# Projections of all token blocks grouped on one weight tile, with one weight load for the group

## The reference

```python
h = rmsnorm(x, norm1_g);  z = h @ w_in            # columns [zb | zc | zv | zu | ga | gs]
ya = zb * conv3_causal(zc * zv)                   # 512 channels
ys, state = s5(zu)                                # diagonal complex state space, 32 groups of 16 channels
gy = gelu(ys);  ys = gy * sigmoid(gy @ w_glu + b_glu)
m = sigmoid(ga) * (ya @ wb_conv) + sigmoid(gs) * (ys @ wb_ssm)
x = x + m @ w_out
h2 = rmsnorm(x, norm2_g);  gate, up = split(h2 @ w_gate_up, 2)
x = x + (silu(gate) * up) @ w_down                # 2816 hidden channels
```

## Time and profile before

| | |
|---|---|
| median of 3 runs | 3663.75 us (3659.91 to 3669.96) |
| profiled execution | 3665.26 us |
| its span, slowest core (core 3) | 3663.7 us |
| spans of the 8 cores | 3647.5 to 3663.7 us, mean clock 0.981 to 0.985 |
| PE busy (matmuls) | 3504.0 us, 96% of the span, 23912 instructions |
| PEld busy (weight loads) | 1979.7 us, 54%, 23912 instructions |
| DVE (VectorE), ACT (ScalarE), POOL (GpSimd) | 44%, 31%, 17% |
| chain that ended last | PE 88%, of which line 669 (`proj`) 83% |

### The profile page before, as it was taken

One profiled execution on the slowest core, in us unless ns is written; L12 is line 12 of the kernel. 1 busy time (PEld: TensorE's weight loads), 2 busy tenths in 40 slices (PEclk: granted clock), 3 DMA queues, 4 the chain that ended last, 5 costly groups with the idle time before them and its releaser, 6 DMA issues.

```text
span 3663.7 us, 67385 instructions; the slowest of 8 cores (3647.5 to 3663.7 us)
## 1 busy us (share of the span) xinstructions
PE 3504.0 (96%) x23912; PEld 1979.7 (54%) x23912; DVE 1618.6 (44%) x2889; ACT 1141.7 (31%) x2151; POOL 608.7 (17%) x799
## 2 busy tenths in 40 slices
PE   6699999999999999999999899999999999999998
PEld 3466666666666666666664344444444444444443
DVE  8745555465454654543244331354224442254313
ACT  4443234332353322533134320243103421042202
POOL 4232210322103221030000200002000110002000
PEclk9799999999999999999999999999999999999999
DMA  7444557435574355854338544574445644474443
GB/s 157 115 82 70 114 139 149 87 66 113 138 155 86 62 113 135 185 110 84 70 71 196 116 77 71 98 169 74 75 77 115 144 70 81 70 146 79 79 72 87
DMA packets 252804, 384.14 MB, mean 105 GB/s; under 512 B 157632, under 2 KB 180800, under 8 KB 246848
## 3 DMA queue, kind: packets, MB, share of 16 engines
q0 software_dynamic: 67968, 243.30, 39.5%
q1 hardware_dynamic: 184512, 136.53, 12.8%
HBM read 567.06 MB, written 56.12 MB: 170 GB/s over the span
## 4 chain that ended last, share of the span: by engine, by line
PE 88%; DVE 4%; issue 3%; DMA 3%; ACT 1%; SPq 1%; DVEq 0%; ACTq 0%; POOL 0%; POOLq 0%
PE ps L669 83%; DMA yT<-X 1%; PE ps L702 1%; PE ps L1107 1%; DVE SC L561 1%; DVE H L726 1%; PE ps L1033 1%; PE ps L908 1%; PE ps L1080 0%; DVE X L1246 0%; DMA scv<-CIN 0%; SPq L632 0%; PE ps L895 0%; DMA X<-xsT 0%; DVE R L1225 0%
## 5 line engine op out<-in xcount | busy, mean ns | idle before, releaser
L669 PE MATMUL ps<-H,RING 128*128 128x512 bf16 (+2 forms) x12160 | 2194.9, 340 | 23.5 <-DVE H L726 9.7
L669 PEld LDWEIGHTS ps<-H,RING 128*128 128x128 bf16 x12160 | 1191.5, 99 | 965.9 <-issue 52.3
L669 PE MATMUL ps<-R,RING 128*128 128x384 bf16 (+2 forms) x6400 | 1162.1, 339 | 19.7 <-DMA R<-dy 11.4
L669 PEld LDWEIGHTS ps<-R,RING 128*128 128x128 bf16 x6400 | 624.2, 98 | 517.8 <-issue 35.4
L656 POOL DMA_DIRECT2D RING<-wpk x472 | 253.0, 537 | 2635.0 <-PE ps L669 2431.7
L1268 DVE TENSOR_TENSOR R<-SC,ps 128x384 bf16<-128x384 f32 (+2 forms) x440 | 255.8, 583 | 786.7 <-PE ps L669 773.6
L1267 ACT ACTIVATE SC<-ps 128x384 f32<-128x384 f32 (+2 forms) x440 | 226.1, 515 | 1208.0 <-PE ps L669 1199.6
L1246 DVE TENSOR_TENSOR X<-X,ps 128x384 f32<-128x384 f32 (+2 forms) x480 | 269.8, 582 | 448.2 <-PE ps L669 445.2
L700 ACT ACTIVATE H<-X 128x384 bf16<-128x384 f32 (+2 forms) x304 | 156.6, 539 | 198.4 <-DVE X L1246 178.7
L726 DVE SCALAR_TENSOR_TENSOR H<-X,PRM,SC 128x384 bf16<-128x384 f32 (+2 forms) x304 | 183.0, 672 | 35.0 <-ACT SC L707 34.8
L1240 POOL TENSOR_TENSOR R<-TB,SC 128x384 bf16<-128x384 f32 (+1 forms) x160 | 168.1, 1063 | 113.1 <-DVE SC L1237 101.4
(11 more groups left out here) (180 smaller groups left out, 1633.1 us busy)
## 6 DMA issues: line engine op xcount, KB each, us to landing
RING<-wpk POOLq DMA_DIRECT2D x440, 512.0 KB, 7.0
TAB<-stash SPq DMA_DIRECT2D x21, 1792.0 KB, 10.0
stash<-TAB SPq DMA_DIRECT2D x15, 1792.0 KB, 7.6
R<-stash SPq DMA_DIRECT2D x7, 1792.0 KB, 14.8
RING<-wpk POOLq DMA_DIRECT2D x32, 384.0 KB, 6.1
du<-R SPq DMA_DIRECT2D x32, 256.0 KB, 9.2
UU<-du SPq DMA_DIRECT2D x32, 256.0 KB, 7.2
dy<-YY SPq DMA_DIRECT2D x32, 256.0 KB, 6.6
```

The source lines that it names most:

```text
L669: subs.append((lambda e, u=u, kw=kw, c=c, src=src, i=i: e.matmul(ps[:, 0:blk.n], lhsT=u.ap(kw, c), rhs=src(blk), start=(i == 0), stop=(i = ...
```

## The change

`proj` takes a list of blocks. For each weight tile it runs the matmuls of all these blocks one after the other: the first in the usual way, with a load, the others through `keep`, which issues a matmul that is told not to load. Each block has a PSUM buffer of its own, and all of them belong to one operation of the scheduler. The planned durations change: `MMW` for a product of one block, `MMK` for matmuls of a group.

All products use the whole list of blocks (`joint`) but for four: zu of the first two row tiles and the first fg/fu unit of a layer go block by block (`split`), and so do wo and the second part of fd. In the convolution, all blocks of zv come first, then all of zc; all of gs come before all of wbb.

```diff
 MMN = lambda n: max(64, n + 6) / 2400.0
+MMW = lambda n: n / 2400.0 + 0.0092 + max(0, 512 - n) * 4.6e-5
+MMK = lambda n: n / 2400.0 + 0.0035
...
-    def proj(parts, blk):
-        ps = PP.new()
+    def keep(e, out, lhsT, rhs, start, stop):
+        return e.add_instruction(mybir.InstMatmult(
+            start_tensor_calc=start, stop_tensor_calc=stop, tile_size=(128, 128), tile_position=(0, 0), ldweights=False,
+            name=nc.get_next_instruction_name(), engine=mybir.EngineType.PE, ins=[e.lower_ap(rhs), e.lower_ap(lhsT)], outs=[e.lower_ap(out)]))
+
+    def proj(parts, bl):
+        pss = [PP.new() for _ in bl]
         nmm = len(parts)
         subs = []
         for i, (u, kw, c, src, keys) in enumerate(parts):
...
+            for bi, blk in enumerate(bl):
+                ps = pss[bi]
+                if bi == 0:
+                    fn = lambda e, u=u, kw=kw, c=c, src=src, i=i, ps=ps, blk=blk: e.matmul(
+                        ps[:, 0:blk.n], lhsT=u.ap(kw, c), rhs=src(blk), start=(i == 0), stop=(i == nmm - 1))
+                else:
+                    fn = lambda e, u=u, kw=kw, c=c, src=src, i=i, ps=ps, blk=blk: keep(
+                        e, ps[:, 0:blk.n], u.ap(kw, c), src(blk), i == 0, i == nmm - 1)
+                subs.append((fn, [u.key] + keys(blk), MMW(blk.n) if len(bl) == 1 else MMK(blk.n)))
+        S.pe(subs, [(ps,) for ps in pss], FULL)
+        return pss
...
         blks = BLKS[half]
+        joint = [blks]
+        split = [[b] for b in blks]
...
             u = next_unit("zu")
+            for bl in (split if f0 == 0 else joint):
+                for mt in range(2):
+                    f = 2 * f0 + mt
+                    for blk, ps in zip(bl, projh(u, mt, bl)):
...
-                    pc, pv = projh(uc, mt, blk), projh(uv_, mt, blk)
+                pvs = projh(uv_, mt, rb_)
+                pcs = projh(uc, mt, rb_)
+                for blk, pc, pv in zip(rb_, pcs, pvs):
...
-                for mt in range(2):
+                for bl, mt in [(b_, m_) for b_ in (split if t0 + pr == 0 else joint) for m_ in range(2)]:
                     ti = slots[2 * pr + mt]
-                    for blk in blks:
+                    for blk, pg, pu in zip(bl, projh(ug, mt, bl), projh(uu, mt, bl)):
```

More of the change, by code:

```diff
@@ L1155, in gas @@
                 t_ = tj[jj] = TP.new()
-                for blk in blks:
-                    pg = projh(uga[jj // 2], jj % 2, blk)
+                for blk, pg in zip(blks, projh(uga[jj // 2], jj % 2, blks)):
                     act(lambda e, t_=t_, pg=pg, blk=blk: e.activation(out=t_[:, blk.c0:blk.c0 + blk.n], in_=pg[:, 0:blk.n], func=AF.Sigmoid),
@@ L1166, in layer @@
                 cin = CP.new()
[L1167 removed]
+                rb_ = blks[::-1]
+                pvs = projh(uv_, mt, rb_)
+                pcs = projh(uc, mt, rb_)
+                for blk, pc, pv in zip(rb_, pcs, pvs):
                     n = blk.n
[L1169 removed]
                     iv = SP_.new()
@@ L1183, in layer @@
                     S.dma("sp", lambda e, cin=cin, f=f: e.dma_start(out=scv[l, :, 64 + 16 * f:80 + 16 * f], in_=cin[:, 1152:1168]), [(cin, 8)], [], 8192)
-                for blk in reversed(blks):
+                pbs = projh(ub, mt, rb_)
+                for blk, pb in zip(rb_, pbs):
                     n, npr = blk.n, blk.np
@@ L1208, in layer @@
                 j = 4 * j4 + jj
-                for blk in blks:
+                for blk, po in zip(blks, projr(uwa, jj * 128, [YA + k for k in range(4)], blks)):
                     n = blk.n
-                    po = projr(uwa, jj * 128, [YA + k for k in range(4)], blk)
                     t_ = tj[jj]
@@ L1217, in layer @@
                 for mo in range(4):
-                    for blk in blks:
+                    for blk, pg in zip(blks, projr(ug, mo * 128, [YS + k for k in range(4)], blks)):
                         n = blk.n
-                        pg = projr(ug, mo * 128, [YS + k for k in range(4)], blk)
                         sg = SP_.new()
@@ L1230, in layer @@
                 j = 4 * j4 + jj
-                for blk in blks:
+                for blk, pg, po in zip(blks, projh(ugs[jj // 2], jj % 2, blks), projr(uwb, jj * 128, [UT + k for k in range(4)], blks)):
                     n = blk.n
-                    pg = projh(ugs[jj // 2], jj % 2, blk)
-                    po = projr(uwb, jj * 128, [UT + k for k in range(4)], blk)
                     sg = SP_.new()
@@ L1273, in layer @@
                     for mt in range(2):
-                        for blk in blks:
-                            parts = [((ua, ub)[k // 8], k % 8, mt * 128, rsrc(slots[k]), rk(slots[k])) for k in range(16)]
-                            xadd(proj(parts, blk), 2 * jq + mt, blk)
+                        parts = [((ua, ub)[k // 8], k % 8, mt * 128, rsrc(slots[k]), rk(slots[k])) for k in range(16)]
+                        for blk, ps in zip(blks, proj(parts, blks)):
+                            xadd(ps, 2 * jq + mt, blk)
             else:
```

17 lines of the change are left out of this document (4 added, 13 removed).

## The result

The changed kernel takes 3776.84 us (median of 4 runs, 3755.2 to 3821.22), the kernel before on the same chips 3665.45; ratio 1.0275, 95% interval 1.0207 to 1.0343. The forecast was 3720 with a range to 3760: the sign was right, the size was not.

The account below looks back on a forecast made before the run. TensorE's stream and its waits were taken as the bound, with loads already hidden. Terms 0 + 19 + 16.5 + 15 + 5.4 + 6 + 4 - 7 - 5 = 53.9 us on 3665.3 gave 3719, say 3720 us; range 3660 to 3760.

Parts of the forecast that it names:

- More half clock: Expected sign: more stretches of TensorE at granted clock 0.50, behind new waits such as those at the norms.
- Loads removed: 9216 matmuls without a load, each saving 0 to 2.6 ns: 0 to 24 us, taken as 0.
- the first rival: Loads do cost, so their removal outweighs the waits from 5.9 ns a matmul; 8.5 ns gives 3642 us; chance 0.12.
- Norm n1, second half: First product behind the norm waits for H tiles with 8 matmuls of cover, not 32: 3 x 5.5 = 16.5 us lost.
- Norm n1, first half: 32 cover matmuls before the third block's first product go; waits for H and half clock: 3 x 6.3 = 19 us.
- State space: Layers 2 to 4: waits for VT, 15 us in the first half; lost gate-matmul cover, 5.4 us in the second.
- wo: At its start, waits for the first block's tile since the last merge product signals once: 8 x 0.7 = 6 us.
- Norm n2, first half: At an existing wait of TensorE, cover shrinks from 64 to 56 matmuls: 1.3 us, three times, 4 us lost.
- Second half, first layer: Wait for the last round's result before glu is covered by 56 matmuls instead of 16: 7 us gained.
- Instruction supply: Waits without a releaser shrink with 9216 instructions fewer: 5 us gained, bounds 0 and 14.
- the start: Start-up, where VectorE sets the pace with the same work: 0, with 10 us either way.
- The third rival: Waits chain up: late table load for the fourth state space round, more half clock; 3754 us, chance 0.18.

Follow-up runs that it names:

- E1: Changed kernel with every matmul loading its weights again, same order and plan; 3760.18 to 3766.78 us, ratio to the kernel before 1.0222.
- E2: Changed kernel with both zu tile pairs, the first products behind norm n1, block by block, all else grouped; ratio to the kernel before 1.0157.
- E3: Changed kernel with the gate and convolution products block by block, all else grouped; ratio to the kernel before 1.0254.
- E5: Changed kernel with GpSimd's next-layer table work started only when norm n2's last H tile is written; ratio to the kernel before 1.0237.
- E8: Changed kernel with the planned matmul durations as before the change, groups kept; ratio to the kernel before 1.0204.
- E7: Changed kernel with the glu products and the merge block by block; ratio to the kernel before 1.0218.
- E4: Grouping in the feed-forward products alone, all else in the order and with the planned durations of the kernel before; ratio to it 1.003.
- E11: Grouping in the feed-forward alone, old planned durations, GpSimd's table work started behind norm n2; ratio to the kernel before 1.0011.
- E12: E11 with groups of at most two blocks; lowest time 3646 us, profiled time 3653 us, -18 and -20 us against the kernel before.
- E10: Changed kernel with old planned durations and with zu, gate and convolution products block by block; ratio to the kernel before 1.0228.

## Why the sign was right and the size wrong

The two lowest runs, 3755.2 and 3757.97 us, lie just inside the range; the loss is still 1.8 times the one that was added up, and two of its terms failed. More half clock, which was forecast, came: the mean granted clock is 0.983 in before (median core) and 0.974 on cores 4 to 7 of the changed kernel.

**Loads removed, 0 of a possible 24: right** (E1: at most 7), and with it falls the first rival. The 25 ns a load, the estimate from the Trainium skill (TensorE: Matmul & The Clock Gate, "Back-to-back issue gap"), do not show at these widths.

**Norm n1, second half, 16.5: right**, 16 us came back in E2. **Norm n1, first half, 19: the wait was there** (2.2 us on line 739 in each layer, then a product drawn out over the tiles), but taking it away returns only 9, since the convolution is the next to be late.

**State space, 15 + 5.4: the waits were there, near the size.** VT waits on core 5 rose from nothing to 13.1 us in half 1, and from 6.5 to 15.1, by 8.6, in half 2. But the covers are not independent: grouping zu alone accounts for 5 of the 13.1 (E2 has 7.7), and E3 takes waits for H away. The norm and the state space together, half 1's layers 2 to 4: 19 + 15 and 2 of wo make 36 predicted, 42 measured; half 2's: 24 predicted, 26 measured.

**wo, 6: 9.0 measured** (eight waits, 1.3 us at most), within its bounds.

```profile
PE ps L679 <- POOL R L1254: 9.0, 8, 1.3
```

**Norm n2, first half, 4: failed.** With the feed-forward and the norm n1 behind it, it is 23.0 - 15.1 + 8.5 = 16.4 us. The step counted matmuls of cover and took the H tiles' durations from the trace of before. It left out that the order of VectorE and GpSimd would move, and that the duration of an H tile depends on what GpSimd does. E5 and E8 both remove the new wait of 6.4 us. E8 does it by the planned durations alone and takes all of the 16.4 back (the three rows are at -3.2), so grouping alone does not cause this loss; the new durations without the groups were not run. The change's two new duration functions had no term in the sum at all; undoing them returns 14 to 22 us. The wait that the step did name, for the third block's H, was 3.2 us in before (core 4, first line) and 4.9 in E8 (core 0, second line), 1.7 longer where 1.3 were forecast; in the changed kernel, behind the new wait, it was 1.5 (core 5).

```profile
PE ps L669 <- DVE H L726: 3.2, 2, 2.4
PE ps L679 <- DVE H L739: 4.9, 2, 3.9
```

**Second half, first layer, -7: failed**, +10.8 measured (-1 to 13 by core). The wait for the last round's result did shrink, by 3.8 us only, from 13.5 to 9.7. The step put the 56 matmuls into the gap and counted no new wait at the places they left. There are such waits now, for the convolution (line 1219), for Y's results (line 1131) and others, and glu itself waits 4.1 us for its sigmoids, where the granted clock is 0.50 (2110 to 2120 us on core 5). E7 shows that the sigmoids' wait and the round's trade one for one; that the others come from the matmuls that moved is argued, not shown.

**Instruction supply, -5:** waits without a releaser on core 5 fell from 13.0 to 9.7 us in the layers behind the first, -3.

The misses: 16.4 - 4 = 12; 10.8 + 7 = 18; 42 - 36 = 6, 26 - 24 = 2; 2 to 3 each at the start, the change of half and the rest, which had 0, together 7; and 5 for the supply, which had no place of its own, so that its gain lies inside these rows. That makes 50, where 101 - 54 = 47 were missing (wo's 1.4 us in the two first layers and the rounding of medians are the difference). The third rival, waits that chain up, has the sign and nearly the time (3754), but by luck: the table load it named shows in no wait of TensorE on core 5.

Open: why layer 4 of half 1 loses 13 to 16 us in E4, E11 and E12 (R comes late by its transfer, 5.6 us in E11, and instruction supply, 3.4), and why fine and coarse products side by side cost layers of half 1 in E3 and E10. That a group keeps its banks longer is supported for the feed-forward alone, by E12, where VectorE's list moved as well.

## What to carry to other kernels

Before saving an instruction, show that it is on the path: if a matmul takes the same 2.6 ns over its columns at three widths, with a load of 98 ns that fills 45% of its time at 512 columns and 84% at 272, the load is hidden there, and what its removal does to the order is the larger part. In a program that a planner orders, every number that the planner reads is an edit of its own: change durations and grouping apart, and compare by stages, since E3's sum of zero was some 50 us won and 55 lost. And look at what a cover is made of: rows of matmuls ahead of a norm, and also free banks, which groups of three use up six at a time.

## What the runs showed of the hardware

Beside GpSimd's work some of VectorE's instructions take much longer: here only ones with all operands in SBUF, and not all of those. Over the eight cores of the changed kernel, instructions alone and with over 80% of their time beside a GpSimd tensor_tensor (median ns, count):

```
scalar_tensor_tensor, 384 columns, X to H (SBUF)    612 (822)     1614 (62)
scalar_tensor_tensor, 272 columns, X to H (SBUF)    496 (434)     1307 (72)
tensor_tensor, 384 columns, one operand in PSUM     549 (2482)     547 (86)
tensor_scalar, 256 columns, one operand (SBUF)      293 (40)      1065 (88)
tensor_tensor, 512 columns, TB to SC (SBUF)         691 (993)      693 (83)
```

The Trainium skill (GPSIMD Engine Reference, "1. Specifications") says that GpSimd shares its SBUF interfaces with VectorE, and that they contend when VectorE's instruction is in a 2-port perf mode or has two SBUF inputs. The trace agrees for the first three rows: 2.6 times as long with two, unchanged with one in PSUM. The fourth has a single input and takes 3.6 times as long; no run here shows whether it is in such a mode. Of the 83 of the last row, which have two, 52 kept 0.7 us and 31 took 1.1 to 2.1. One of the 52 stands in the changed kernel's timeline above: VectorE's had started at 289.65, 0.04 us ahead of GpSimd's, and took 0.69 us, while GpSimd's took 1.58, where the same instruction with VectorE idle takes 1.07 (median of 120).
